# A sorted table of token numbers for the 64 experts, and four buffers for gathered rows

## The reference, cut to what matters

```python
scores = jax.nn.sigmoid((t @ w_router))            # 512 tokens x 64 experts
...                                                # group-limited choice
_, eidx = lax.top_k(jnp.where(emask, biased, -jnp.inf), TOP_K)      # 8 of 64 for each token
w = jnp.take_along_axis(scores, eidx, axis=-1)
w = w / jnp.sum(w, axis=-1, keepdims=True) * ROUTED_SCALE
...
hw = jax.nn.silu(t @ w_gate[e]) * (t @ w_up[e]) * combine[:, e]     # 1024 -> 256, per expert
routed = routed + hw @ w_down[e]                                    # 256 -> 1024
shared = (jax.nn.silu(t @ ws_gate) * (t @ ws_up)) @ ws_down         # one expert for all tokens
```

## Time and profile before

| | |
|---|---|
| median of 3 runs | 1147.69 us (1137.47 to 1148.98) |
| profiled execution | 1155.55 us, its span 1153.6 us |
| busy share PE, DVE, ACT, POOL | 89%, 82%, 51%, 27% |
| first store of an expert issued | 425.45 us |
| last store of an expert issued | 1146.76 us |

### The profile page before, as it was taken

How to read it: one execution, slowest core, us unless ns; L and a number is a source line. 1 busy time by engine, 2 the same in 40 slices (tenths; PEclk the granted TensorE clock), 3 DMA queues, 4 the chain that set the end, 5 groups by cost and what they waited for, 6 DMA issues and landing times.

```text
span 1153.6 us, 15762 instructions
## 1 busy us (share of the span) xinstructions
PE 1023.9 (89%) x4842; PEld 800.1 (69%) x4843; DVE 940.2 (82%) x1484; ACT 592.3 (51%) x884; POOL 311.3 (27%) x183
## 2 busy tenths in 40 slices
PE   3796989897998989989898999999898998988985
PEld 1363484676887768778777877777787877777774
DVE  3678679545557579999998998999999998999984
ACT  1122251556022247657665765666666666666662
POOL 0005005400000113424333432333434243334231
PEclk9898999878999999999999998999999999999998
DMA  9975401200048269999998998999999999999972
GB/s 316 393 257 205 146 9 73 92 1 1 19 184 298 84 236 336 347 314 306 316 299 288 317 325 291 310 313 326 327 307 313 315 321 328 334 300 337 318 248 54
DMA packets 86182, 285.60 MB, mean 248 GB/s; under 512 B 18036, under 2 KB 18548, under 8 KB 77064
## 3 DMA queue, kind: packets, MB, share of 16 engines
q1 hardware_dynamic: 64240, 248.03, 60.6%
q0 software_dynamic: 19008, 35.71, 12.4%
q10 hardware_dynamic: 2904, 1.48, 0.5%
HBM read 280.94 MB, written 37.75 MB: 276 GB/s over the span
## 4 chain that ended last, share of the span: by engine, by line
DMA 45%; PE 35%; DVE 9%; issue 6%; POOL 2%; ACT 1%; SPq 1%; POOLq 0%; DVEq 0%; ACTq 0%
DMA out<-oute,dst_i 35%; DMA xe<-h_rows,src_i 8%; PE bank L553 5%; PE bank L554 5%; PE bank L555 5%; PE bank L612 5%; PE bank L687 2%; PE bank L766 2%; POOL out L512 2%; DMA ada_w<-in_w_ada 2%; DVE ada_acc L1209 2%; PE bank L704 2%; PE bank L815 2%; DVE q_sb L1288 1%; PE bank L695 1%
## 5 line engine op out<-in xcount | busy, mean ns | idle before, releaser
L1442 DVE TENSOR_TENSOR gu_low<-w_gu,gu_high 128x1024 fp32r<-128x1024 f32 x256 | 301.5, 1220 | 14.5 <-ACT gu_high L1082 8.4
L1082 ACT CAST gu_high<-w_gu 128x1024 fp32r<-128x1024 f32 x256 | 256.4, 1054 | 101.8 <-PE bank L555 96.0
L512 POOL DMA_INDIRECT out<-oute,dst_i x64 | 151.0, 2360 | 455.3 <-DMA out<-oute,dst_i 266.0
L553 PE MATMUL bank<-gu_high,xeT_high 128*128 128x512 f32 x512 | 206.6, 404 | 0.0
L555 PE MATMUL bank<-gu_high,xeT_low 128*128 128x512 f32 x512 | 201.2, 393 | 0.0
L554 PE MATMUL bank<-gu_low,xeT_high 128*128 128x512 f32 x512 | 200.5, 392 | 0.0
L1442 DVE TENSOR_TENSOR d_low<-w_d,d_high 128x1024 fp32r<-128x1024 f32 x128 | 150.5, 1217 | 0.0
L1088 ACT CAST d_high<-w_d 128x1024 fp32r<-128x1024 f32 x128 | 128.2, 1055 | 12.4 <-PE bank L555 12.4
L1093 ACT CAST xeT_high<-bank 128x512 fp32r<-128x512 f32 x128 | 68.8, 590 | 112.9 <-PE bank L815 112.9
L506 POOL DMA_INDIRECT xe<-h_rows,src_i x64 | 108.3, 1692 | 65.2 <-issue 39.3
L815 PE MATMUL bank<-ident,xe 128*128 128x128 f32 x512 | 75.4, 293 | 54.1 <-DMA xe<-h_rows,src_i 53.9
(11 more groups left out here) (262 smaller groups left out, 1454.4 us busy)
## 6 DMA issues: line engine op xcount, KB each, us to landing
w_gu<-in_w_exp_gate SPq DMA_DIRECT2D x128, 512.0 KB, 5.3
w_gu<-in_w_exp_up SPq DMA_DIRECT2D x128, 512.0 KB, 9.2
w_d<-in_w_exp_down SPq DMA_DIRECT2D x64, 1024.0 KB, 9.1
ada_w<-in_w_ada SPq DMA_DIRECT2D x12, 2048.0 KB, 11.6
w_out_sb<-in_w_out SPq DMA_DIRECT2D x2, 2048.0 KB, 7.2
w_lat_sb<-in_w_in SPq DMA_DIRECT2D x1, 2688.0 KB, 21.9
x_sb<-in_x SPq DMA_DIRECT2D x1, 2048.0 KB, 23.9
w_v_sb<-in_w_in SPq DMA_DIRECT2D x1, 2048.0 KB, 10.3
```

The costliest lines, as they stand in the source:

```text
L512: pool.indirect_dma_start(out_rows, bass.IndirectOffsetOnAxis(ap=dst_i[i][:], axis=0), oute[i][:], None, bounds_check=last_row, oob_is_err ...
L553: pe.matmul(dst, xh, wh, start=start, stop=False)
L1082: act.copy(gu_high[half][:, m], w_gu[half][i][:, m]).then_inc(gu_high_ok[half], 1)
L1442: return dve.tensor_tensor(low, whole, high.bitcast(F32), ALU.subtract)
```

## The change

A sorted table of token numbers takes the place of compare and product per expert. After the choice of experts, DVE writes `keys` = (1024 - token number) where a token has the expert and 0 elsewhere; PE transposes them, so that partition `h*64 + e` holds the 256 tokens of half `h` for expert `e`. Sixteen rounds of `max` (the eight largest) and `match_replace` on 128x256 elements list them in order of token number. The list is transposed back, and the second half of the tokens is laid in reversed: first half in slots 0, 1, 2, ..., second half in slots 127, 126, 125, ...; `src_tab` holds the row numbers of all 64 experts. `one_hot`, `indices` and `index_rows` stay only for further blocks. The weights of the 64 experts are stored behind each row in DRAM, so a gathered row has 1088 instead of 1024 numbers, and ACT copies the expert's one out of it (`row_weights`). `xe` has four buffers, so `gather(e+3)` waits for `rows_T(e-1)`; POOL's steps are written out for all 64 experts. In the prologue the shared expert's parts are ordered anew around the sixteen rounds.

```diff
+            pool.wait_ge(wts_ok, 1)
+            pool.dma_start(h2_dram.rearrange("(t p) d -> p t d", p=P)[:, :, D:D + NE], wts[:]).then_inc(st_w, 16)
             pool.wait_ge(h2T_tr, 2 * T)
...
+            pool.wait_ge(src_ok, 1)
+            pool.wait_ge(st_w, 16)
+            for e in range(3):
+                if e == 2:
+                    pool.wait_ge(sgu_mm, T)
+                gather(src_tab[:, e:e + 1], e)
...
+            for e in range(NE):
+                g = e + 3
+                if g < NE:
+                    if e:
+                        pool.wait_ge(xeT_tr, e)
+                        pool.wait_ge(w_ok, e)
+                    gather(src_tab[:, g:g + 1], g % 4)
+                pool.wait_ge(oute_ok, e + 1)
+                if e:
+                    pool.wait_ge(st_y, 16 * e)
+                scatter(src_tab[:, e:e + 1], e % 2)
...
             def step(E):
-
-                if exists(after(E, 3)) and not first(E):
-                    indices((E[1] + 3) % 2, num(E, 3), num(E, 3))
                 hidden_T(E[1] % 2, num(E))
...
+            def row_weights(E):
+                b = E[1] % 4
+                act.wait_ge(ld_xe[b], times(fours(E), 16))
+                act.copy(slots[b][:, 1:2], xe[b][:, bass.ds(num(E, D), 1)]).then_inc(w_ok, 1)
...
-                dve.tensor_scalar(dst_i[i][:], slots[j][:, 0:1], BIG, None, ALU.add)
...
+            dve.wait_ge(key_tr, 1)
+            for r in range(P // 8):
+                best = found[:, 8 * r:8 * r + 8]
+                now = bank[0][:, 0:2 * P] if r == 0 else left[:]
+                ins = dve.max(best, now)
+                if r == P // 8 - 1:
+                    ins.then_inc(found_ok, 1)
+                    break
+                link(ins)
+                link(dve.match_replace(left[:], best, now, 0.0))
+                if r == 3:
+                    shared_hidden(0)
+                if r == 7:
+                    shared_hidden(1)
+                if r == 11:
+                    shared_out(0)
+
+            dve.wait_ge(found_tr, 1)
+            dve.tensor_copy(found_T[:], bank[1][:, 0:P]).then_inc(foundT_ok, 1)
+            shared_hidden(2)
+            dve.wait_ge(flip_mm, 1)
+            dve.wait_ge(foundT_ok, 1)
+            link(dve.scalar_tensor_tensor(later[:], found_T[:, 0:NE], 0.0, bank[1][:, P:P + NE], ALU.is_equal, ALU.mult))
+            link(dve.tensor_tensor(later[:], later[:], found_T[:, 0:NE], ALU.add))
+            dve.tensor_scalar(src_tab[:], later[:], -1.0, LAST, ALU.mult, ALU.add).then_inc(src_ok, 1)
...
             def step(E):
-                E1, E2, E3, E4 = (after(E, d) for d in (1, 2, 3, 4))
-                if exists(E3) and not first(E):
-                    wait(dve, oute_ok, num(E))
-                    index_rows(E3[1] % 4, num(E3))
+                E1, E2 = after(E, 1), after(E, 2)
                 hidden_low(num(E))
-                if exists(E4) and not first(E):
-                    one_hot_of(E4)
```

More of the change, by code:

```diff
@@ L239, in trunk_kernel @@
         nmax = small("nmax", [P, T, H])
-        src_i = [small(f"src_i{i}", [P, 1], I32) for i in range(4)]
+        src_x = small("src_x", [P, 1], I32)
         slots = [small(f"slots{i}", [P, 2]) for i in range(4)]
-        dst_i = [small(f"dst_i{i}", [P, 1], I32) for i in range(2)]
         list_i = small("list_i", [P, 2 * MAXX], I32)
@@ L271, in trunk_kernel @@
         ld_d = [sem("ld_d0"), sem("ld_d1")]
-        ld_xe = [sem("ld_xe0"), sem("ld_xe1")]
+        ld_xe = [sem(f"ld_xe{i}") for i in range(4)]
         gu_high_ok = [sem("gu_high0_ok"), sem("gu_high1_ok")]
@@ L515, in _ @@
             pool.wait_ge(h2T_tr, 2 * T)
-            for r in range(3):
-                pool.wait_ge(idx_ok, r + 1)
-                if r == 2:
-                    pool.wait_ge(xeT_tr, 1)
-                gather(r % 4, r % 2)
-            def step(E):
-                G = after(E, 3)
-                if exists(G):
-                    pool.wait_ge(idx_ok, num(G, 1))
-                    pool.wait_ge(xeT_tr, num(G, -1))
-                    gather(G[1] % 4, G[1] % 2)
-                if first(E):
-                    for t in range(T):
-                        pool.wait_ge(sh_ok, t + 1)
-                        pool.dma_start(out_rows[t * P:(t + 1) * P, :], x[:, t]).then_inc(st_x, 16)
-                    pool.wait_ge(st_x, 16 * T)
-                pool.wait_ge(oute_ok, num(E, 1))
-                wait(pool, st_y, times(num(E), 16))
-                scatter(E[1] % 2)
@@ L845, in rows_T_of @@
             def rows_T_of(E):
-                rows_T(E[1] % 2, times(pairs(E), 16), num(E))
+                rows_T(E[1] % 4, times(fours(E), 16), num(E))
             def gate_up_of(E):
                 gate_up(E[1] % 2, num(E), num(E, -1))
+            pe.wait_ge(ld["wsh"], 32)
+            pe.wait_ge(x1_ok, 2 * T)
+            shared_gu(0)
+            shared_gu(1)
+            pe.wait_ge(key_ok, 1)
+            for s in range(2):
+                last = pe.transpose(bank[0][:, s * P:(s + 1) * P], keys[:, s].rearrange("p h e -> p (h e)"), ident[:])
+            last.then_inc(key_tr, 1)
+            pe.wait_ge(sco_ok, 1)
+            for t in range(T):
+                for t2 in range(t + 1):
+                    pe.matmul(bank[6][:, t * NE:(t + 1) * NE], tri[:] if t2 == t else ones[:], selm[:, t2, :], start=(t2 == 0), stop=(t2 == t))
+            for t in range(T):
+                last = pe.matmul(bank[6][:, T * NE:(T + 1) * NE], ones[:], selm[:, t, :], start=(t == 0), stop=(t == T - 1))
+            last.then_inc(pos_mm, 1)
             shared_hT(0)
@@ L1525, in _ @@
             last.then_inc(lmat_ok, 1)
-            index_rows(2, 2)
-            one_hot_of((None, 3))
+            dve.wait_ge(lmat_ok, 1)
+            shared_out(2)
+            rows_low_of((None, 0))
+            shared_out(3)
+            gate_up_low_of(0, (None, 1))
+            rows_low_of((None, 1))
+            gate_up_low_of(1, (None, 1))
+            down_low(0, 0)
+            dve.wait_ge(shT_tr, T)
+            hidden(0, 0, 0)
+            gate_up_low_of(0, (None, 2))
+            gate_up_low_of(1, (None, 2))
             dve.wait_ge(list_mm, 1)
```

235 lines of the change are left out of this document (109 added, 126 removed).

## The result

| | before | after |
|---|---|---|
| median of the runs | 1148.34 us (1137.47 to 1155.58) | 1115.14 us (1105.86 to 1126.00) |
| ratio, with its 95% interval | | 0.970 (0.964 to 0.976) |
| profiled execution, its span | 1155.55 us, 1153.6 us | 1113.93 us, 1112.0 us |
| first store issued | 425.45 us | 424.71 us |
| 61st store issued | 1120.69 us | 1079.82 us |

The change makes the kernel 3.0% faster: 33 us by the medians, 41.6 by the profiled spans. The 60 steps give 695.24 - 655.11 = 40.1 us of the 41.6; the first store goes 0.7 us earlier, and what follows the 61st is 0.7 shorter. The forecast was 1091.

A forecast was written before the change was run, and what follows sets the result against it. Each store's wait for the last one's landing was taken to bound the loop. 422 + 60 x 10.7 + 25.5 + 6.8 = 1096 us of span against 1153.6, -57, so 1091 from the median; 8-in-10 range 1048 to 1138.

The forecast's parts named there:

- What bounds the kernel: Expert loop: each store waits for the last one's landing, 10.8 us in the mean; DVE (10.72) and PE (10.31) don't bind.
- The step: Expert loop: rows at both ends of the slots relieve loaded DMA engines, so a step falls from 11.59 to 10.7 us.
- even bound of 10.1: Loop transfers, rows evenly dealt over the engines: 7.95 us of weights + 2.10 + 0.06 = 10.1 us a step.
- The removed work: Loop: DVE loses 0.79 us and PE 0.92 us a step; taken alone worth nothing, the step stays 11.59.
- rival (c): POOL's store writing meets DVE's splits: 1.5 us more per landing, +90 us, 1237; or 2.0 us rounds, 1153 to 1160; chance 0.10.
- The spread: Store and gather rows at both slot ends: 12.15 us on loaded engines today, 10.1 if evenly dealt; 10.7 taken.
- Buffers, POOL's loop, the wider row: POOL and gathers: four buffers worth nothing, 0.81 us landing-to-issue falls by 0 to 0.2, rows 6% longer cost 0.06 us.
- The prologue: Before the loop: sixteen rounds of 1.0 us, half hidden; first store at 422 us, plus or minus 6, instead of 425.45.
- Rival (a): Loop: a store's landing is not relieved, step 11.4 to 11.6 us, 1138 to 1148 us; chance 0.13.
- Rival (b): Loop: full relief, DVE becomes the bound, step 9.95 to 10.2 us, 1051 us from the median; chance 0.15.

The follow-up runs named there:

- the even deal: Changed kernel plus one small product that deals each expert's tokens out over the slots: 1097.43 us, ratio 0.962 to the kernel before; run again, 1097.56 us, 0.960.
- without any chain: Changed kernel with dealt slots, each expert's rows stored to an array of its own so stores don't wait for the last: 1092.58 us, ratio 0.953 to before.
- a_packed: Changed kernel with all of an expert's tokens in the slots from 0 up, as before the change: 1150.21 us, ratio 0.999 to the kernel before.
- after_side: The changed kernel run once more, unchanged, beside the dealt-slots kernel on one chip: 1122.87 us, ratio 0.982 to the kernel before.
- b_halves: Kernel before with only the slot numbering changed, even places in the lower 64 slots, odd in the upper: 1133.35 us, ratio 0.990 to before.
- the control: Kernel before with places 0 to 63 kept in the lower 64 slots but dealt out over the groups there: 1136.10 us, ratio 0.990 to before.
- a_work: Changed kernel with the like of DVE's removed operations put back in each step, results unused: 1155.81 us, ratio 1.017 to the kernel before.
- a_two: Changed kernel with two buffers for gathered rows instead of four: 1114.40 us, ratio 0.979 to the kernel before.

## Why the prediction was right and wrong

**What bounds the kernel.** Right. The landing of the store before set the step, and does so after the change too, in 49 stores of the stretch. The rate rose from 317 to 338 GB/s (forecast: towards 340) and the share from 0.95 to 0.99. The 266 us that the prediction read from the page understate the wait before the change, by the stores put down to `slots`.

**The step.** Forecast 10.7 us, measured 10.92. The term that was mis-sized is the landing. I had it at 9.9 us; it is 10.15. 60 x 0.22 = 13 us of the 16 that separate the span (1112.0) from the forecast one (1096). The even bound of 10.1 was not reached even with the even deal (10.53 to 10.58) nor without any chain (10.50). It priced the weights at the rate that they had alone, 7.95 us a step, though my own count from the queues had 8.87 for the same bytes. After the change that count is 0.611 x 1112.0 / 248.03 = 2.74 us for each MB of weights and 0.132 x 1112.0 / 36.89 = 3.98 for POOL's, of which a step moves (36.89 - 2.10 - 0.13) / 64 = 0.54 MB (0.13 are the stored weights): 3.15 x 2.74 + 0.54 x 3.98 = 10.8 us, 0.99 of 10.92. By the profiles the engines' time for a step thus hardly fell (from 10.97), and what went away is mostly time in which they stood idle. The lower bound of the sum was too low by some 0.4 us, and taking a value near the middle of the bounds carried that error over.

**The other 8 us.** Between 1091 and 1115 lie 24 us, and the span accounts for 16. I took the difference of 57 us, counted from a profiled execution 8 us above the median, off the median; the forecast span of 1096 by itself meant an execution of 1098.

**The removed work.** "Taken alone worth nothing" held: without the spread it brings nothing beyond the spread of the runs (`a_packed`, 0.999). What failed is its price beside the spread, and that is the main miss, though the total hides it. I had priced 0.79 us of DVE's work against DVE's own slack, 11.59 - 10.72, and wrote that with the work in place 10.72 would bind. With it in place the step is 11.57: it costs 11.57 - 10.92 = 0.65 us, as good as all of the loop's gain. Its way to the critical path is, for the greater part, POOL: the store's instruction is on that path in full, since its length is contained in the landing, and it is held up by DVE's instructions with two operands in SBUF. I had this mechanism in hand as rival (c), and used it only for what it might add, not for what it already cost before: 2.36 us in the earlier trace rows where 1.56 is the free time. Of the 0.60 us that the landing lost, 0.39 is the write (2.40 to 2.01) and 0.21 the rest; with `after_side` in place of the first profile it is 0.24 and 0.43, so how the two share it is open. My step ascribed all of it to the transfer. That the time came out within the range owes something to luck: of two parts that each take the gain along when they are left out, I had counted on one.

**The spread.** The mechanism stood: rows at both ends land sooner, 0.48 us of a step (`a_packed`), and in the kernel before 1.0% of the time (`b_halves`). That this is the doing of the two halves is not shown: the control, with the first 64 places on the lower one, gained as much. I also forecast that the deal "will not be quite even", and the more even one was worth another 0.34 us, if it was the evenness. The parts don't add up: in the kernel after, either of the two, the spread or the lighter DVE, has little effect without the other (11.40 and 11.57, where both have 10.92). That `a_work` has 11.57 and `b_halves` 11.24 (1.017 and 0.990), with a spread and some 0.79 us of such work on DVE in both, stays open. 0.27 of these 0.33 us lie in the write (2.58 and 2.31), which points to when stores meet DVE's splits; which part of the order decides that, I haven't shown. Nor is it shown why TensorE's granted clock from 450 to 1040 us is 0.96 in `a_work`, where the kernels before and after have 0.98 and `b_halves` 0.99, and whether that costs anything.

**Buffers, POOL's loop, the wider row.** Four buffers at nothing: right (`a_two`). The 0.8 us from landing to issue stayed (10.92 - 10.15 = 0.77). Bytes of q0 grew from 35.71 to 36.89 MB, 3%, as the 6% of half of them says.

**The prologue.** The round was right: 0.98 to 1.00 us for a forecast 1.0. The sum was not. It is best counted from `selm`, since the part ahead of it, which the change doesn't touch, happened to end 4.05 us earlier (348.33, in the earlier trace rows 352.38): from `selm` to the first store it is 73.07 us before and 76.38 after, 3.3 longer where I forecast 3.4 shorter. (The repeat agrees: 432.44 - 356.08 = 76.36 in `after_side`.) The list took 29.5 us to `src_tab` where I had 28.1: the transposition fell behind `shared_down(1)` on PE. The larger part came behind it, from `src_tab` to the first store: 46.8 against 41.5, with two waits that I had not placed, `shared_down(3)` for `x_sb` (2.42) and `down(0)` for `hwT_low` (2.65). DVE, which got 15 us of rounds, was the engine on which both stood. The first store at 424.71 lies in the forecast's 416 to 428 only by the earlier start.

**Rival (a)** (landing not relieved): fell, 10.15 against 10.75. **Rival (b)** (DVE becomes the bound at 9.95 to 10.2): fell; no run went under 10.50, and what stops it there is open. **Rival (c)**: in the changed kernel it went the other way, the mean write fell from 2.36 to 2.015 us and not over 2.55. But in `a_work` the mean is 2.555 and the kernel is slower than before: the mechanism was right, the sign for this change was not, as the work that meets POOL was being taken away. That the mean there equals the 2.55 of the forecast is a coincidence.

## What to carry to other kernels

An instruction that issues a transfer on the critical path is part of that path: when its mean is well above its shortest (here 2.36 against 1.56 us), ask which DVE instructions it meets before you price work removed from DVE at nothing. Where a gather or scatter fills only some of its slots, deal the live rows out over the partitions; one permutation gave 2.3% here, beside the 3.0% of the whole change. And where two parts relieve one chain, try the kernel without each: here, taking out either one left nothing of the 3.0% (ratios 0.999 and 1.017).

## What the hardware showed that I had not expected

- 0.79 us of DVE's work, with which DVE needs 10.74 us a step, brought the step from 10.92 to 11.57; 0.41 of these 0.65 us went away when one operand of one 0.68 us instruction lay in PSUM.
- A store's instruction that is issued while a pair of splits runs ends 1.46 us after the pair, whether it was issued 0.47 or 0.24 us into it. It takes 3.35 and 3.57 us in place of 1.55 to 1.58. With the compare right ahead of the pair it takes 4.23; with one operand of the compare in PSUM, 1.58.
- The order of the rows over the slots moves a store's landing without its write from 8.47 to 7.56 us (7.47 in the repeat), at the same bytes and the same instructions.
- No version of the loop moved more than 351 GB/s of weights and rows together, with the DMA engines' share at 0.99 to 1.01, where weights alone had 396.
- Another order of the first 64 places within the lower 64 slots helped as much as using both halves (11.19 against 11.24 and 11.13 us; ratios 0.990, 0.990 and 0.986). I have no explanation that a run shows.
